# Two of three token tiles' routing weights: from one-hot products on TensorE to 4-byte indirect adds in memory

## The reference, cut to what matters

```python
def chunk(xc):                                    # 128 tokens
    q = (xc @ w_q).reshape(128, 8, 2, 128)
    s1 = einsum('thd,nd->thn', q[:, :, 0], k1)    # 128 keys each
    s2 = einsum('thd,nd->thn', q[:, :, 1], k2)
    v1, i1 = top_k(s1, 16); v2, i2 = top_k(s2, 16)
    cand = v1[..., :, None] + v2[..., None, :]    # 256 candidates
    cand_id = i1[..., :, None] * 128 + i2[..., None, :]
    top_s, top_pos = top_k(cand, 16)
    ids = take_along_axis(cand_id, top_pos)
    g = softmax(top_s)
    act = einsum('thkd,td->thk', u[ids], xc)
    w = g * gelu(act)
    return einsum('thk,thkd->td', w, v[ids])
```

## Time and profile before

| | us |
|---|---|
| median of three runs | 3612.45 (3610.29 to 3612.54) |
| profiled execution, its own time | 3611.08 |
| its span, first to last instruction | 3609.3 |
| TensorE matmul busy | 3531.3 (98%) |
| VectorE busy | 2708.6 (75%) |
| ScalarE busy | 1417.4 (39%) |
| GpSimd busy | 962.2 (27%) |
| TensorE on the chain that ended last | 69% |

### The profile page before, as it was taken

The page is one execution under the profiler, slowest core; times in us unless marked ns, Lnnn a source line. Parts: engine busy times, 40 slices in busy tenths (PEclk is TensorE's granted clock), DMA queues, the critical chain, the costliest instruction groups (busy, mean ns, idle before and its releaser), DMA issues.

```text
span 3609.3 us, 56050 instructions
## 1 busy us (share of the span) xinstructions
PE 3531.3 (98%) x19806; PEld 3150.9 (87%) x19806; DVE 2708.6 (75%) x5629; ACT 1417.4 (39%) x1857; POOL 962.2 (27%) x601
## 2 busy tenths in 40 slices
PE   7999999999999999999999999999999999999998
PEld 7888788999999987777888887889999999877777
DVE  5665448999986588888766644399999965888887
ACT  5554333434443333333355533333344433333333
POOL 1000003551112244444200000135511122544442
PEclk9999999999999999999999999999999999999999
DMA  3112322468888999999721133225777798999996
GB/s 143 47 46 105 130 97 94 160 252 299 299 297 316 329 349 374 371 378 379 281 83 47 46 122 135 100 80 168 279 296 294 291 332 323 366 363 375 365 382 245
DMA packets 217388, 851.64 MB, mean 236 GB/s; under 512 B 19504, under 2 KB 69056, under 8 KB 168496
## 3 DMA queue, kind: packets, MB, share of 16 engines
q1 hardware_dynamic: 120944, 478.99, 36.8%
q0 software_dynamic: 74432, 270.53, 20.3%
q10 hardware_dynamic: 21888, 100.67, 6.8%
HBM read 747.36 MB, written 102.76 MB: 236 GB/s over the span
## 4 chain that ended last, share of the span: by engine, by line
PE 69%; issue 12%; DVE 9%; DMA 4%; ACT 3%; POOL 3%; ACTq 0%; DVEq 0%; SPq 0%; POOLq 0%; PEldq 0%
PE bank L1294 16%; PE bank L1047 15%; PE bank L1049 15%; PE bank L1048 15%; PE bank L1269 5%; DMA raw<-in_stream 4%; POOL lo L393 3%; DVE h L962 3%; DVE lo L671 3%; PE bank L1156 1%; ACT hi L421 1%; PE bank L1133 1%; DVE act_in L1000 1%; ACT w_hi L634 1%; PE bank L1146 1%
## 5 line engine op out<-in xcount | busy, mean ns | idle before, releaser
L671 DVE TENSOR_TENSOR lo<-raw,hi 128x2048 fp32r<-128x2048 f32 x308 | 705.2, 2290 | 374.5 <-ACT hi L421 373.2
L1047 PE MATMUL bank<-xT_hi,hi 128*128 128x384 f32 (+1 forms) x2688 | 950.4, 354 | 5.7 <-DVE lo L671 2.4
L1049 PE MATMUL bank<-xT_hi,lo 128*128 128x384 f32 (+1 forms) x2688 | 935.7, 348 | 0.0
L1048 PE MATMUL bank<-xT_lo,hi 128*128 128x384 f32 (+1 forms) x2688 | 934.0, 347 | 0.0
L421 ACT ACTIVATE hi<-raw 128x2048 fp32r<-128x2048 f32 x356 | 682.1, 1916 | 353.9 <-PE bank L1294 193.2
L1294 PE MATMUL bank<-hi,w_hi 128*128 128x512 f32 x1536 | 611.5, 398 | 6.2 <-DVE w_lo L1002 5.9
L1294 PE MATMUL bank<-hi,w_lo 128*128 128x512 f32 x1536 | 608.9, 396 | 0.0
L1294 PE MATMUL bank<-lo,w_hi 128*128 128x512 f32 x1536 | 608.8, 396 | 0.0
L1047 PEld LDWEIGHTS bank<-xT_hi,hi 128*128 128x128 f32 x2688 | 505.2, 188 | 38.7 <-issue 11.6
L410 POOL DMA_INDIRECT rows<-in_u_rows,ids x256 | 303.1, 1184 | 851.8 <-DVE act_row L959 795.0
L1049 PEld LDWEIGHTS bank<-xT_hi,lo 128*128 128x128 f32 x2688 | 504.4, 188 | 26.0
(11 more groups left out here) (195 smaller groups left out, 4807.2 us busy)
## 6 DMA issues: line engine op xcount, KB each, us to landing
raw<-in_stream SPq DMA_DIRECT2D x356, 1024.0 KB
act_d<-act_s ACTq DMA_DIRECT2D x128, 384.0 KB
gate_d<-gate_s ACTq DMA_DIRECT2D x24, 2048.0 KB
gate_in<-gate_d SPq DMA_DIRECT2D x32, 1536.0 KB
act_in<-act_d SPq DMA_DIRECT2D x128, 384.0 KB
rows<-in_u_rows,ids POOLq DMA_INDIRECT x256
rows<-in_v_rows,ids POOLq DMA_INDIRECT x256
h<-in_x SPq DMA_DIRECT2D x1, 2048.0 KB, 9.4
```

Source lines behind the costliest of these rows:

```text
L671: dve.tensor_tensor(lo[s][:], raw[s][:], hi[s][:].bitcast(F32), ALU.subtract).then_inc(lo_done, 1)
L1047: pe.matmul(dst, a_[0], b_[0], start=first, stop=False)
L1048: pe.matmul(dst, a_[0], b_[1], start=False, stop=False)
L1049: return pe.matmul(dst, a_[1], b_[0], start=False, stop=last)
```

## The change

Tile 0 keeps the one-hot products (`HOT` = 1): 32 groups a layer, one a step, instead of 96, three a step. For tiles 1 and 2 (`SCAT` = 2) a new table `gate_sd` in memory takes their place. ScalarE's queue fills it with zeros from `zero_r` in 16 DMAs of 1 MB a layer, one a step during the mixer's merge. VectorE computes a flat address for each picked expert of each token (`s_idx`). GpSimd then issues 256 indirect DMAs a layer (8 heads x 2 tiles x 16 picks), each of which adds 128 elements of 4 bytes, one from each partition, to the table. They stand in GpSimd's order as three adds and then one row fetch. At the start of each head's 16 adds of a tile it waits for that tile's adds before them. GpSimd's share of `lo` ends three chunks earlier, at chunk 13, and VectorE begins at chunk 14, behind its lookups. Row operations are two a step from step 16 and three a step from step 56. SyncE's queue waits for all adds ahead of chunk 58. In the v stage the table comes in two loads (0.5 MB and 1 MB) and VectorE multiplies in two instructions instead of one.

```diff
-EXP_STEP, IDX_STEP = 8, 12
+EXP_STEP, IDX_STEP = 8, 14
-G_RING, G_PER_STEP, G_TOK = 4, 3, 4
-GROUPS = TD // G_TOK
+G_RING, G_PER_STEP, G_TOK = 4, 1, 4
+HOT = 1
+SCAT = NDT - HOT
+GROUPS = HOT * P // G_TOK
-G_ROWS, TAIL_ROWS = 2, 2
+DVE_STEP = 13
+SCATS_PER_ROW = 3
+SCATTERS = SCAT * P
+def rows_at(st):
+    return 0 if st < FIND_STEPS else 2 if st < C_U - 8 else 3
...
+    gate_sd = nc.dram_tensor("gate_sd", (SCAT, P, P * P), F32, kind="Internal").ap()
...
+        flat_gates = gate_sd.rearrange("x j (f o) -> (x j f) o", o=1)
+        zeros = zero_r[:].bitcast(F32).unsqueeze(1).broadcast_to([P, P * P // T // ZERO_PARTS, T])
...
# SyncE's queue
-                load_weights(0, P_V - 5)
+                load_weights(0, P_V - 3)
+                for x in range(SCAT):
+                    wait_alone(sp, scattered[x], 16 * P * (l + 1), sp_passed)
...
                 load_gates(0, 0, first=True)
-                load_weights(P_V - 5, P_V - 3)
+                load_weights(P_V - 3, P_V - 2)
                 load_gates(1, 1, first=True)
...
# GpSimd
-                with pool.Fori(1, C_WQ // 2 + J_G) as j:
+                with pool.Fori(1, C_WQ // 2 + DVE_STEP // 2) as j:
...
-                split_lo(lp + P_U + J_G, 0)
+                for c in range(DVE_STEP // 2 * 2, DVE_STEP + 1):
+                    split_lo(lp + P_U + c // 2, c % 2)
...
+                def scatter(n):
+                    hd, x, k = n // (SCAT * TOPK), n // TOPK % SCAT, n % TOPK
+                    if k == 0 and hd + l > 0:
+                        wait_alone(pool, scattered[x], 16 * (P * l + TOPK * hd), pool_passed)
+                    k += hd * TOPK
+                    pool.indirect_dma_start(flat_gates, bass.IndirectOffsetOnAxis(s_idx[:, x, k:k + 1], 0),
+                                            s_g[:, x, k:k + 1], None, compute_op=ALU.add).then_inc(scattered[x], 16)
...
+                for n in range(SCATTERS):
+                    scatter(n)
+                    if n % SCATS_PER_ROW == SCATS_PER_ROW - 1:
+                        fetch_row(fetched)
+                        fetched += 1
...
# VectorE
-                for tt in range(NT):
+                for o, tt in enumerate((*range(HOT, NT), *range(HOT))):
...
+                    elif tt >= HOT:
+                        x = tt - HOT
+                        looked(dve.scalar_tensor_tensor(out=idx_t[:, tt, 1], in0=idx_t[:, tt, 1], scalar=P,
+                                                        in1=idx_t[:, tt, 0], op0=ALU.mult, op1=ALU.add))
+                        dve.tensor_scalar(s_idx[:, x], idx_t[:, tt, 1], P, lane[:, x:x + 1], ALU.mult, ALU.add).then_inc(s_ready, 1)
```

More of the change, by code:

```diff
@@ L82 @@
 SLICE = 32
-SLICES = TD // SLICE
+SLICES = HOT * P // SLICE
 PER_SLICE = SLICE // G_TOK
@@ L88 @@
 ROW_OPS = 2 * P
-G_ROWS, TAIL_ROWS = 2, 2
-U_ROW_OPS = G_ROWS * G_STEPS + TAIL_ROWS * (C_U - FIND_STEPS - G_STEPS)
+DVE_STEP = 13
[3 more added lines that the diff above has]
+    return 0 if st < FIND_STEPS else 2 if st < C_U - 8 else 3
+U_ROW_OPS = sum(rows_at(st) for st in range(C_U))
 V_ROW_OPS = ROW_OPS - U_ROW_OPS
@@ L272, in build @@
         row_gelu, row_weighed = sem("row_gelu"), sem("row_weighed")
+        s_ready, zeroed = sem("s_ready"), sem("zeroed")
+        scattered = [sem(f"scattered{x}") for x in range(SCAT)]
         rows_in = [sem(f"rows_in{r}") for r in range(NR)]
@@ L529, in _ @@
                         ahead(p, s)
+                        if m < ZERO_PARTS:
+                            part = P * P // ZERO_PARTS
+                            act.dma_start(gate_sd[bass.ds(j, 1), :, m * part:(m + 1) * part].rearrange("x j (a b) -> j (x a) b", b=T),
+                                          zeros).then_inc(zeroed, 16)
                         act.wait_ge(w_used, 2 * p + s + 1 + CR)
@@ L620, in _ @@
                     ahead(lp + P_U + j, s)
[L621 to L629, removed]
+                    gelu(j, s, 0)
+                    g_evac(st)
+                    gelu(j, s, 1)
+                    store_act(j, s)
+                    if st % PER_SLICE == PER_SLICE - 1:
+                        store_gates(st // PER_SLICE)
                 def weights_hi(k, s):
@@ L931, in lookup @@
                     dve.tensor_reduce(idx_t[:, tt, half], look, AX.X, ALU.add).then_inc(idx_done, 1)
-                for tt in range(NT):
[L934 to L939, removed]
-                        dve.scalar_tensor_tensor(out=ids[:], in0=idx_t[:, tt, 0], scalar=P, in1=idx_t[:, tt, 1],
-                                                 op0=ALU.mult, op1=ALU.add).then_inc(ids_done, 1)
-                    if tt == 0:
+                for o, tt in enumerate((*range(HOT, NT), *range(HOT))):
+                    lookup(o, tt, 0)
+                    lookup(o, tt, 1)
+                    if o == 0:
                         dve.wait_ge(exp_ready, l + 1)
@@ L982, in _ @@
                             t = slice(q * G_TOK + r, q * G_TOK + r + 1)
-                            o = onehot[:, q % G_RING, r]
-                            dve.tensor_scalar(o[:, 0], iota[:], idx1T[:, t], gT[:, t], ALU.is_equal, ALU.mult)
-                            last = dve.tensor_scalar(o[:, 1], iota[:], idx2T[:, t], None, ALU.is_equal)
+                            hot = onehot[:, q % G_RING, r]
+                            dve.tensor_scalar(hot[:, 0], iota[:], idx1T[:, t], gT[:, t], ALU.is_equal, ALU.mult)
+                            last = dve.tensor_scalar(hot[:, 1], iota[:], idx2T[:, t], None, ALU.is_equal)
                         last.then_inc(oh_done, 1)
-                    ahead(p, s)
-                    for _ in range(G_ROWS if st < G_STEPS else TAIL_ROWS):
+                    ahead(lp + P_U + st // 2, st % 2)
+                    for _ in range(rows_at(st)):
                         row_op(n)
```

76 lines of the change are left out of this document (50 added, 26 removed).

## The result

| | before | after |
|---|---|---|
| median of all runs, us | 3611.37 (3609.0 to 3612.54, 4 runs) | 4169.99 (4166.86 to 4177.61, 4 runs) |
| ratio of the medians | | 1.155 (95%: 1.1531 to 1.1571) |
| span of the profiled execution, us | 3609.3 | 4175.8 |

The kernel became 558.6 us slower. I had forecast 3873, with 3600 to 4150: the sign is right, the loss is more than twice what I said, and the time lies outside the range.

The account below looks back on a forecast made before the run. TensorE bounded the kernel before; GpSimd's 341 indirect DMAs (443 us) plus 112 held would then set the pace. With the table's end, the v stage starts 131 us later a layer: 3611.1 + 261, median 3873, range 3600 to 4150.

Parts of the forecast that it names:

- TensorE's gain: u stage: with fewer one-hot products and GpSimd keeping up, the v stage starts at 1214.5, 43.8 us earlier a layer.
- The standstill at step 14: u stage: TensorE stands still for 17 us until VectorE's `lo` of chunk 14 is ready behind the lookups.
- The hold: u stage: GpSimd is held while VectorE runs `lo` or a row operation, 2.67 us a step, 112 us a layer.
- the fetch at 776.68: GpSimd's row fetch of 3.62 us, begun during VectorE's `lo`, read as ending 0.95 us after the first row operation.
- The upper bound: GpSimd's pace in the u stage at 1.48 us per DMA plus 112 us held: v stage at 1451, 3997 us in all.
- the DMA rival: u stage: the DMA engines are the bound, 14.9 us a step, 4035 us and up; chance 0.17.
- the rival's point: u stage: 0.12 us of DMA engine time per added element, the point given for the DMA engines being the bound.
- Not held by VectorE: u stage: GpSimd runs unhindered beside VectorE, adds end at 1209, v stage starts +37 us, 3648 in all; chance 0.15.
- Cheap adds: GpSimd in the u stage: adds break even at 0.79 us each, full gain of 3524 at 0.62; chance 0.18.
- The table's end: End of u stage: 18 us from the last add to step 58, then six steps of 8.32 us to the v stage.
- The clock: u stage: TensorE's gaps may lower its granted clock, but slower products fit into 3.8 us spare a step; nothing.
- The rows moved to the u stage: v stage: 152 row operations instead of 160, entered at nothing.

Follow-up runs that it names:

- no_adds: The changed kernel with every add and the waits for adds left out, so two tiles' weights stay zero: 3508.95 us, ratio 0.972.
- one_input_row_op: The changed kernel with the u stage's row operation as a tensor_reduce over the fetched row, without the product with x: 4053.12 us, ratio 1.123.
- bench_issue: A separate kernel timing 12 GpSimd DMAs of each kind, alone and beside eight VectorE instructions: alone, row fetch 0.94 us, add 1.54, plain scatter 0.96.
- late_table_wait: The changed kernel with SyncE's wait for the adds and the first table loads moved behind the loads of chunks 58 to 61: 4156.06 us, ratio 1.151.
- one_hots_three_times: The changed kernel with each one-hot product of tile 0 done three times over into the same bank: 4163.72 us, ratio 1.152.
- no_adds_96_rows: The changed kernel without adds and with two row operations in the last eight u steps, 96 u-stage rows instead of 104: 3520.27 us, ratio 0.975.

## Why the prediction was right in direction and wrong in size

The step that failed is "I take 1.00 + 0.30 = 1.30 for both kinds. An add addresses 128 places as a fetch does, and its nearest row is that fetch." A plain scatter to the same places does cost what a fetch costs, 0.96 + 0.30, but an add costs 1.54 + 0.30. The rest of the working, for layer 0:

| term | predicted | measured |
|---|---|---|
| first add, us | 766 | 765.4 |
| 85 fetches and their gaps (86 measured) | 111 | 81 + 26 |
| 256 adds and their gaps | 333 | 394 + 78 |
| held by VectorE | 112 | 128 |
| last add issued | 1321 | 1471 |
| from there to the v stage | 68 | 78 |
| v stage's start, later than before | +131 | +290.7 |
| v stage's own length | 0 | -6.8 |

The 128 is what the two groups are busy beyond the unheld prices: 438.2 - 256 x 1.54 = 44 and 164.5 - 86 x 0.94 = 84 (a fetch between adds took up to 1.00, with which it would be 5 less). The adds are 139 of the missing 160 us a layer, the holds 16, the tail 10, and the fetches give back a few.

- *TensorE's gain* was right: 1214.5 against 1215.5 in no_adds. The standstill at step 14 was 14.8 us where I said 17.
- *The hold* was right in kind and about right in size, and it was shown in the kernel (one_input_row_op) and by itself (bench_issue). One reading of mine was off: the fetch at 776.68 ended at 780.30, 0.83 us and not 0.95 after the first row operation; nothing hangs on it.
- *The upper bound* of 3997 was made of the mean of all u fetches, 1.18 us. It is the price of the wrong operation. No row of the kernel before showed an accumulate, and for an operation without a row a bound from another kind of operation is no bound. What I widened the range by came from the DMA rival, and ended 20 us short.
- *The DMA engines as the bound* fell: a share of 0.59 over the stretch. Its price per element can be worked out as well. The indirect queue's packets took 0.223 x 16 x 4175.8 / 148192 = 0.101 us on average. In no_adds the same queue has 74464 packets at 21.0% of 3507.1 us, which is 11784 us in all; the kernel after has 14899. The 73728 packets more, 144 an add of 128 elements, cost 0.042 us each, or 0.048 an element, and the rival's point was 0.12. This is an estimate: it takes the fetches' own packets as equally dear in both kernels. The Trainium skill's 0.2 us for an HBM access ("DMA: Bandwidth & Descriptors", Latency and other measured facts), put on every element with nothing overlapped, is not what this trace shows.
- *Not held by VectorE* fell: beside tensor_tensor an add took 1.84 to 3.12 us and a fetch 1.86 to 2.40, where 1.54 and 0.94 stand alone. The Trainium skill ("SBUF — State Buffer", Who interferes with whom) infers that tensor_tensor leaves descriptor writing alone; here the trace disagrees. Its rule that tensor_reduce never contends agrees: 1.54 beside it.
- *Cheap adds* fell: the point was 0.79 us an add with its gap, and it was 1.84. The direct DMA from which I took this rival does have its gap in its 0.54 us: 12 took 6.53 us from start to end.
- *The table's end* was 10 us larger than said: step 58 began at 1495.7, 24 us after the last add where I had 18, and the six steps from there took 53 us and not 50. And late_table_wait shows that I had its cause half wrong: the order of the queue matters less than the bytes, which all come due together once the last add has landed.
- *The clock*: the granted clock was 0.81 in the stretch, where TensorE has gaps in every step. It was entered at nothing, and one_hots_three_times agrees: with three times the products TensorE was busy 66.47 us of the 90 (900 to 990), at a granted clock of 0.89, still with room to spare.
- *The rows moved to the u stage* were entered at nothing and gave 5.5 of the 6.8 us of the v stage (no_adds_96_rows).

The plain scatter freed 334 us and half the adds 536, where the prices alone give 297 and 472. Both times the held part shrank as well, from 128 us a layer to 106 and 101, which is 44 and 54 us in all and brings the sums to 341 and 526. What stays open is why it shrank: how the holds fall when GpSimd's and VectorE's orders shift against each other was not measured by itself. Open as well is which property of a VectorE instruction holds GpSimd, the second input or the full result.

## What to carry to other kernels

Price an indirect DMA by what its engine does to issue it, and measure that for the very form that you want: the same 128 places cost 0.94 us to fetch, 0.96 to scatter and 1.54 to add, and 512 times 0.60 is 307 of the 559 us. When work goes from the busiest engine to one that was waiting, first count what that engine then has to do in one step and add what its neighbour holds it for (here 6 adds and 2 fetches: 706 us over 42.7 steps, 16.5 each, of which 3 are holds, against the 9.24 that TensorE needs). A small move in the same change, eight rows a layer from the v stage to the end of the u stage, paid 0.2% by itself, and sixteen paid nothing.

## What the runs showed of the hardware

- An indirect DMA of 128 places on GpSimd: fetch 0.94 us for rows of 4 KB and 0.95 for 4 bytes, plain scatter 0.96, add 1.54, add from 64 partitions 1.42, each with 0.30 us to the next. Direct DMAs on the same queue: 0.54 us each with no gap between them (6.53 for 12).
- Beside VectorE's tensor_tensor on 128x2048, one indirect DMA gets through per VectorE instruction (2.20 us), be it an add or a fetch. tensor_reduce holds none (1.54); tensor_scalar on f32 holds (2.16 to 3.10), eight in 9.18 us, with three adds held.
- By estimate, a packet of an accumulating DMA took 0.042 us of a DMA engine, and an add of 128 elements of 4 bytes has 144 packets, as worked out above.
